# The modulation vectors' partial sums: four transposes and a VectorE sum in place of four products with a selector

## The reference, cut to what matters

```python
c_act = silu(c)                                    # layer 1
mod = (c_act @ w_ada + b_ada)                      # 1024 -> 6144
sh1, sc1, ga1, sh2, sc2, ga2 = split(mod, 6)
h = rmsnorm(x, ln1_pre) * (1 + sc1) + sh1          # needs the first two sections
proj = h @ w_in                                    # 11 blocks of 256 columns in the kernel

mod = silu(c_2) @ w_ada_2 + b_ada_2                # layer 2, the same with its own weights
mod_ctx = silu(c_ctx) @ w_ada_2[:, :2*d] + b_ada_2[:2*d]
```

## Time and profile before

| | |
|---|---|
| three runs, median (lowest, highest) | 2075.65 us (2071.66, 2075.8) |
| profiled execution, span | 2059.7 us |
| median less span (what lies around it) | 15.95 us |
| PE busy | 1877.4 us, 91%, 13222 instructions |
| DVE busy | 856.6 us, 42%, 1997 |
| ACT busy | 553.5 us, 27%, 1028 |
| chain that ended last, by engine | PE 76%, DMA 15%, DVE 5%, ACT 2% |
| chain, by line | L254 31%, L1764 18%, L1838 9%, loads of w_ada 4%, L414 2%, L436 1% |

### The profile page before, as it was taken

The page is one execution under the profiler, slowest core; times in us unless marked ns, Lnnn a source line. Parts: engine busy times, 40 slices in busy tenths (PEclk is TensorE's granted clock), DMA queues, the critical chain, the costliest instruction groups (busy, mean ns, idle before and its releaser), DMA issues.

```text
span 2059.7 us, 32420 instructions
## 1 busy us (share of the span) xinstructions
PE 1877.4 (91%) x13222; PEld 1273.1 (62%) x13223; DVE 856.6 (42%) x1997; ACT 553.5 (27%) x1028; POOL 475.5 (23%) x523
## 2 busy tenths in 40 slices
PE   5999999879888899999999999989999999999766
PEld 3778788844444588677666668456656556565322
DVE  3144634353321432622777322344344444443226
ACT  4132512411211342413667203111111111111111
POOL 1000000032221100010554000115445544545320
PEclk9999999979999999889999999999999999999998
DMA  8655541379999641232777242379999999999877
GB/s 340 247 209 201 205 184 62 154 287 415 417 417 411 247 151 66 82 62 94 151 146 124 81 178 89 144 271 397 394 366 412 412 406 393 411 397 412 316 281 305
DMA packets 103193, 532.33 MB, mean 258 GB/s; under 512 B 28082, under 2 KB 28386, under 8 KB 48380
## 3 DMA queue, kind: packets, MB, share of 16 engines
q1 hardware_dynamic: 64208, 457.73, 56.1%
q0 software_dynamic: 36256, 64.54, 11.7%
q10 hardware_dynamic: 2572, 7.81, 1.1%
HBM read 524.34 MB, written 51.90 MB: 280 GB/s over the span
## 4 chain that ended last, share of the span: by engine, by line
PE 76%; DMA 15%; DVE 5%; ACT 2%; issue 2%; SPq 0%; POOL 0%; ACTq 0%; POOLq 0%; DVEq 0%
PE ps L254 31%; PE ps L1764 18%; PE ps L1838 9%; DMA arena<-in_egu 9%; DMA arena<-in_ada 4%; PE ps L1730 3%; PE ps L414 2%; PE ps L3065 1%; PE ps L1825 1%; PE ps L436 1%; DMA arena<-h_rows,arena 1%; PE ps L3091 1%; PE ps L1086 1%; PE ps L2293 1%; DMA arena<-y_rows 1%
## 5 line engine op out<-in xcount | busy, mean ns | idle before, releaser
L1764 PE MATMUL ps<-arena 128*64 128x256 f32 x4096 | 480.0, 389 | 47.3 <-DMA arena<-in_egu 37.4
L1764 PEld LDWEIGHTS ps<-arena 128*64 128x64 f32 x4096 | 296.3, 140 | 249.7 <-issue 61.3
L254 PE MATMUL ps<-arena 128*128 128x256 f32 (+4 forms) x1268 | 319.6, 411 | 13.0 <-issue 5.3
L254 PEld LDWEIGHTS ps<-arena 128*128 128x128 f32 (+1 forms) x1268 | 221.7, 198 | 94.2 <-issue 67.6
L1712 POOL DMA_INDIRECT arena<-h_rows,arena x160 | 191.8, 1199 | 272.2 <-DVE arena L1704 116.9
L1838 PE MATMUL ps<-arena 128*64 128x512 f32 x1024 | 242.3, 602 | 7.0 <-DVE arena L1833 3.0
L1718 POOL DMA_INDIRECT y_rows<-arena x160 | 160.2, 1001 | 377.6 <-DVE arena L1869 320.8
L1833 DVE COPY arena<-ps 128x256 f32<-128x256 f32 (+1 forms) x96 | 36.5, 380 | 399.3 <-PE ps L1825 399.3
L1812 ACT ACTIVATE arena<-ps 128x256 f32<-128x256 f32 (+1 forms) x96 | 33.5, 349 | 489.2 <-PE ps L1764 489.2
L3029 POOL DMA_DIRECT2D arena<-in_nabias x160 | 85.4, 541 | 304.7 <-PE ps L2907 177.6
L1838 PEld LDWEIGHTS ps<-arena 128*64 128x64 f32 x1024 | 66.2, 136 | 101.8 <-issue 96.7
(11 more groups left out here) (433 smaller groups left out, 2743.1 us busy)
## 6 DMA issues: line engine op xcount, KB each, us to landing
arena<-in_egu SPq DMA_DIRECT2D x204, 1024.0 KB, 15.4
arena<-in_ed SPq DMA_DIRECT2D x102, 1024.0 KB, 14.9
arena<-in_ada SPq DMA_DIRECT2D x48, 1024.0 KB, 7.0
arena<-in_win SPq DMA_DIRECT2D x37, 1024.0 KB, 5.0
arena<-y_rows SPq DMA_DIRECT2D x20, 1024.0 KB, 16.0
arena<-in_nabias POOLq DMA_DIRECT2D x96, 128.0 KB, 5.7
arena<-in_wout SPq DMA_DIRECT2D x8, 1024.0 KB, 7.3
h_rows<-arena ACTq DMA_DIRECT2D x8, 512.0 KB, 3.4
```

The source lines that it names most:

```text
L254: z = pe.matmul(o, l, r, start=start and i == 0, stop=stop and i == len(pairs) - 1, skip_group_check=check)
L1764: z = pe.matmul(b[64 * j:64 * j + 64, 256 * s:256 * s + 256], XV[:, c, 64 * h:64 * h + 64], wk(k)[:, j * 256:j * 256 + 256], start=k == 0, ...
```

## The change

The four products with the selector become four transposes of the same four 128x128 pieces of MS, which fill 512 columns of the bank in place of 4 or 8. VectorE then reads one column of each of the four groups (and, in layer 2, of each of the two halves in a group), that is 16 or 32 numbers per partition, and sums over the four groups with a `tensor_reduce`; a second instruction adds the bias, in place, and waits for the first. The bank is free again after the sum (key "added"), no longer after the bias. The order of all other instructions stays.

```diff
         def pe_ada_fold(pe, w, n, order=None):
-            width = ADA[PAIRS[n][0]][3]
-            b = banks.turn(ada, ("fold", n), ("mod", n), order)
+            b = banks.turn(ada, ("fold", n), ("added", n), order)
             for f in b.free:
                 w.wait_ge(*f)
             w.wait_ge(*ada.to("ms", n))
             for c in range(4):
-                z = pe.matmul(b.ap[:, c * width:(c + 1) * width], MS[n % 2][:, c * 128:(c + 1) * 128], SEL[:, 0:width],
-                              start=True, stop=True)
+                z = pe.transpose(b.ap[:, c * 128:(c + 1) * 128], MS[n % 2][:, c * 128:(c + 1) * 128], ident)
             z.then_inc(*ada.up("pe", "fold", n))
...
         def dve_ada(dve, w, n):
...
-            dve.tensor_tensor(cut(MOD[:, c0 * width:(c0 + 4) * width], 4),
-                              cut(banks.of(ada, "fold", n).ap[:, 0:4 * width], 4),
-                              bc(bias[:, c0:c0 + 4].unsqueeze(2), [128, 4, width]), ALU.add).then_inc(*ada.up("dve", "mod", n))
+            v = cut(MOD[:, c0 * width:(c0 + 4) * width], 4)
+            turned = banks.of(ada, "fold", n).ap.rearrange("p (c q j r) -> p c j q r", c=4, q=4, j=width)
+            dve.tensor_reduce(v, turned[:, :, :, :, 0], AXX, ALU.add).then_inc(*ada.up("dve", "added", n))
+            w.wait_ge(*ada.to("added", n))
+            dve.tensor_tensor(v, v, bc(bias[:, c0:c0 + 4].unsqueeze(2), [128, 4, width]), ALU.add).then_inc(*ada.up("dve", "mod", n))
```

## The result

| | before | after |
|---|---|---|
| runs | 2069.52, 2071.66, 2075.65, 2075.8 us | 2051.45, 2053.72, 2053.9, 2060.08 us |
| median | 2073.65 us | 2053.81 us |
| ratio, 95% interval | 1 | 0.9925 [0.9898, 0.9953] |
| profiled execution: span | 2059.7 us | 2052.0 us |
| profiled execution: its own time | not listed | 2053.9 us |

The change is 15 us quicker by the ratio, twice the 8.1 us forecast, and 2053.81 lies outside the range of 2062.5 to 2073. The two medians lie 19.8 us apart, from four runs each; the ratio is another estimate from the same runs, and experiment 8 repeats it with more. Yet the two profiles differ by 7.7 us only: the forecast of the span was 2051.6 and the profile has 2052.0. Both facts are true, and the study is about what lies between them.

A forecast was written before the change was run, and what follows sets the result against it. The chain of waits up to 291 us was taken as the bound, folds holding 7.7% of its first 300 us. 6.7 (folds) + 1.4 (start) = 8.1 us; span 2051.6 plus 15.95 gives 2067.5 us, range 2062.5 to 2073.

The forecast's parts named there:

- Two passes for a product, one for a transpose; 0.45 us per fold: Each fold on TensorE: eight records, 0.91 us, become four transposes, 0.46 us, saving 0.45 us.
- 15 of 24 folds on the path, 6.7 us: In win1, 15 folds lie on the chain of waits, the others hide beside loads: 15 x 0.45 = 6.7 us.
- the start 1.4 us: Folds 0 to 3, before the first w_in product: 1.4 us won, middle of 0.6 and 2.3.
- the high end: At the start, the clock rises 3.4 us sooner, L280 ends 2.7 us sooner, and the start wins 2.3 us.
- the load at 41 us: At the start, a load landing at 41.1 lets the last products that use it come only 1.4 us sooner.
- The load margin at 232 us: The load issued at 225.5 lands at 232.1, needed at 232.9; its margin of 0.8 us shrinks to 0.4 and holds.
- VectorE's extra step: The sum behind each fold: 0.19 us each, 0.4 us late in the start, nothing for the 22 behind it.
- the 15.95 us between span and median: Added to the forecast span of 2051.6 us to give the forecast time of 2067.5 us.
- the clock gives more: Rival: 128-column folds keep two stretches at 2.4 GHz, another 2 x 1.6 to 2 us won, 2064 us; chance 0.09.
- The page on transposes and the clock: Skill page says full clock does not engage for transposes; by it the start wins 0.6 us, the whole 7.3.
- The clock takes it back: Rival: longer load waits idle TensorE, 1.6 us per stretch falling to 1.2 GHz; seven give 2079 us; chance 0.05.
- the loads take half of it back: Rival: varying landings or more hidden folds leave 4.0 us of gain, 2071.7 us; chance 0.14.

The follow-up runs named there:

- experiment 8: The change, unchanged, timed once more against the kernel before: ratio 0.9926 [0.9902, 0.995], 15.3 us.
- hidden_more: The change with each transpose of folds 4, 6, 8, 10 and 18 issued four times: ratio to the kernel before 0.9958 [0.9936, 0.998].
- doubled transposes: The change with each transpose issued twice, so TensorE's fold is as long as before: ratio to the kernel before 0.9972 [0.9955, 0.999].
- wide products: The kernel before with each selector product streaming its one or two columns 128 or 64 times: ratio to the kernel before 0.9962 [0.9941, 0.9983].
- experiments 1 to 3: The kernel before unchanged against itself, 0.9988; the same profiled again, 2074.24 us; the kernel before with the change in pieces 0 to 3 alone, 0.999.
- path_more: The change with each transpose of folds 5, 7, 9, 11 and 13 issued four times: ratio to the kernel before 1.0011 [0.9989, 1.0033].

## Why the prediction was wrong, point by point

- *Two passes for a product, one for a transpose; 0.45 us per fold.* Right: 192 records became 96, 0.91 became 0.42 us.
- *15 of 24 folds on the path, 6.7 us; the start 1.4 us.* Right in sum, as far as can be told: 7.8 us at the last fold against the first profile of before and 4.8 in the second profile of the change, 8.5 in the timed kernel that has short folds alone. Of its parts, the start won 0.9 us up to the first product in the first pair of profiles, less than executions of before differ there (46.02 to 47.42). The clock rose sooner than the high end assumed, but the load at 41 us held TensorE back as said. Folds 8, 10 and 18 are less well hidden than assumed (hidden_more).
- *The load margin at 232 us "shrinks to 0.4 and holds".* It didn't hold. In the change the load issued at 220.86 takes 7.76 us to land, against 6.6, and TensorE waits for it; in the second profile the wait is 0.26 us. It cost little:

```profile
228.66 1.07 PE L414 MATMUL ps<-arena 128*32 128x256 f32 x16 [0.81 <-DMA arena<-in_ada]
```

- *VectorE's extra step costs 0.4 us in the start and nothing behind it.* The step is 0.17 to 0.18 us, and the chain of the change's first profile goes through L446 and L448 at 45 us alone; in the second it does so once more, at 231.2, for 0.2 us. Right as far as profiles tell. The doubled transposes (0.9972) and the wide products (0.9962) differ by VectorE's step, the earlier bank and passes; 2 us, inside the intervals.
- *"With the 15.95 us between span and median that is 2067.5."* This is the step that put the time out of the range. I took median less span for what lies around an execution. It is 1.9 to 2.5 us (2053.9 - 2052.0, 2072.91 - 2070.4), and 1.8 to 3.6 over all timed runs of before. So the profiled execution of before took about 2062 us, and it stood at the quick end of a kernel whose runs reach from 2059 to 2082. The forecast span of 2051.6 (measured: 2052.0) should have become 2053.5, close to the measured median of 2053.81. That agreement is luck: a quick execution of before was set against an ordinary one of the change, and the clock's gain, which the sum lacks, was already inside the quick one.
- *The rival "the clock gives more" with 0.09, at 2064.* Here lies why the forecast gain is half of the measured one. The sum put the clock at nothing, and the rival was mis-sized: 3.2 to 4 us were given it, at two places seen in the trace; the wide products, which change no time of TensorE's folds, measured 7.9 us. It was priced from the stretches that were slow in one execution. The place that matters most, 197 to 228 us, ran at full clock in that execution and so had no row. Two of the reasons were there to be seen: TensorE's clock does change in these stages, and 16 us between span and median is far more than a launch needs to explain.
- *The page on transposes and the clock.* The Trainium skill, TensorE: Matmul & The Clock Gate, "Part 4: PE-mode transpose", says that the full clock does not engage for transposes, since they don't count as busy in the same way. The runs say otherwise for these float32 transposes: in the kernel before L280 came from 0.2125 to 0.097 us each after 5.1 us of transposes alone, and in the change it runs at 2.4 GHz from 31.91 on, behind eight transposes. The doubled transposes were quicker than before, at the same time on TensorE.
- *The clock takes it back.* Didn't happen. The waits for w_ada loads grew from 27.5 to 32.2 us in total (9 and 13 waits), twice the 2.25 us forecast, and the clock was no lower for it (mean over the runs 0.966 against 0.963 in experiment 8).
- *A slip in the working.* For "the loads take half of it back" the prediction says 3.7 us more lost; its own terms give 8.1 - 4.0 = 4.1. The 2071.7 is worked out from 4.0 and stands.

What stays open: why the long low spell occurs in one execution of before and not in the next; why it lasts 17 us with TensorE busy; what the wide products gave beyond the estimated 4.7 us of the clock; and how the effect of 128 columns is shared out between the folds. The three profiles of executions over 2070 us with narrow folds in that stretch (experiments 1 to 3) have the spell. The other eleven profiles don't, path_more's among them, whose execution took 2071.21 us.

## What to carry to other kernels

Compare the profiled execution's own time with the timed runs before summing from it: if they are far apart, ask which kind of execution you are reading, and take a second profile. A small TensorE instruction, of up to 128 columns here, costs by its records and not by its columns: a float32 product of one column or of 128 costs 0.114 us twice, a transpose of 128 columns 0.105 to 0.116 once. And where TensorE runs at 1.2 GHz in some executions, what its small instructions stream is worth an experiment of its own: the same time with more columns won 0.4% here (0.2 to 0.6).

## What the runs showed of the hardware that was not expected

- The same program has executions that differ by 10 us in one stretch of 31 us with the granted clock (0.50 in 24 us of it, 1.00 throughout in the other). The two were profiled at different times; on one chip alone its runs reach from 2062 to 2077 us.
- Streaming the same one or two selector columns 128 or 64 times costs no time (0.91 us per fold either way) and made the kernel 7.9 us quicker. The 32 transposes behind the first of these folds took 3.8 us in place of 5.3 to 6.3.
- A two-column product in the fast float32 format and a 128-column transpose hold TensorE nearly equally long, 0.47 and 0.42 us for four: at this size the columns don't set the pace.
